# A decoder stack on one core: four attention units in flight in owned PSUM bank pairs, and projection pairs split in equal halves

## The reference, cut to what matters

```python
# first block, per layer (x: 512 x 1024)
h = rmsnorm(x, g_mix)
dq, dk, dv, c_q, c_kv_kr, xq, gate_logits = split(h @ w_in)
y_diff = diff_attention(...)    # 8 heads, 2 softmax maps each, causal; out = map0 @ v - lam * map1 @ v
y_mla  = latent_attention(...)  # 8 heads of 96, queries and keys from a latent projection, causal
y_mem  = memory_cross_attention(...)  # 4 heads of 128 over 256 rows of memory, no mask
x = x + (sum of gates * (y @ w_o)) @ w_out
x = x + square(relu(rmsnorm(x) @ w_mlp1)) @ w_mlp2
# second block, per layer
p = split(rmsnorm(x) @ w_in)
# four mixers: sparse attention with an index of chosen keys (dsa), attention in three
# branches (compressed keys, selected, windowed), a short convolution, pooled means
x = x + (concatenation of the four, each gated) @ w_out
```

## Time and profile before

| what | value |
|---|---|
| median of 3 executions | 3046.03 us (3041.13 to 3048.8) |
| the profiled execution, its own time | 3044.45 us |
| its span in the profile | 3042.7 us |
| PE, matmul | 2788.1 us busy (92%) |
| POOL | 1955.5 us (64%) |
| DVE | 1165.3 us (38%) |
| ACT | 732.8 us (24%) |
| mean granted TensorE clock | 0.961 of full speed |

### The profile page before, as it was taken

How to read it: one execution, slowest core, us unless ns; L and a number is a source line. 1 busy time by engine, 2 the same in 40 slices (tenths; PEclk the granted TensorE clock), 3 DMA queues, 4 the chain that set the end, 5 groups by cost and what they waited for, 6 DMA issues and landing times. The chain is left out here.

```text
span 3042.7 us, 38827 instructions
## 1 busy us (share of the span) xinstructions
PE 2788.1 (92%) x14268; PEld 2256.7 (74%) x14268; DVE 1165.3 (38%) x1936; ACT 732.8 (24%) x1417; POOL 1955.5 (64%) x1562
## 2 busy tenths in 40 slices
PE   6988999999899997989899999899998999989997
PEld 5766777778788886667777778788887876777765
DVE  4278273311210113278173320310012387426773
ACT  3220454200130201221365210220111114212250
POOL 5767421788798895877420788788896772266704
PEclk9999999999999998999899999999998999989998
DMA  4312100233233333322100233223333321042202
GB/s 120 94 52 66 51 8 8 80 94 96 72 96 97 95 96 82 106 70 67 54 8 1 70 87 97 80 87 96 96 97 88 92 77 32 28 93 73 80 1 69
DMA packets 158902, 217.26 MB, mean 71 GB/s; under 512 B 51312, under 2 KB 62832, under 8 KB 158704
## 3 DMA queue, kind: packets, MB, share of 16 engines
q1 hardware_dynamic: 119952, 209.72, 23.6%
q10 hardware_dynamic: 38752, 4.95, 1.3%
HBM read 212.52 MB, written 2.10 MB: 71 GB/s over the span
## 5 line engine op out<-in xcount | busy, mean ns | idle before, releaser
L290 POOL TENSOR_TENSOR weight_parts<-weight_ring,zero 128x512 fp32r<-128x512 f32 x760 | 863.4, 1136 | 853.4 <-PE ps L375 453.0
L293 POOL TENSOR_TENSOR weight_parts<-weight_ring,weight_parts 128x512 fp32r<-128x512 f32 x780 | 1077.7, 1382 | 62.8 <-ACT weight_parts L301 2.6
L377 PE MATMUL ps<-h_feature_major_high,weight_parts 128*128 128x512 f32 x2304 | 584.6, 393 | 19.5 <-DVE h_feature_major_low L471 6.6
L377 PEld LDWEIGHTS ps<-h_feature_major_high,weight_parts 128*128 128x128 f32 x2304 | 430.4, 189 | 124.8 <-POOL weight_parts L290 11.2
L375 PE MATMUL ps<-weight_parts,h_feature_major_high 128*128 128x512 f32 (+1 forms) x1920 | 463.0, 381 | 34.5 <-DVE h_feature_major_low L1613 9.1
L375 PEld LDWEIGHTS ps<-weight_parts,h_feature_major_high 128*128 128x128 f32 x1920 | 341.8, 194 | 119.0 <-issue 21.9
L377 PE MATMUL ps<-h_feature_major_low,weight_parts 128*128 128x512 f32 x1152 | 309.4, 390 | 0.0
L375 PE MATMUL ps<-weight_parts,ut_high 128*128 128x512 f32 x1024 | 254.6, 390 | 0.0
L377 PEld LDWEIGHTS ps<-h_feature_major_low,weight_parts 128*128 128x128 f32 x1152 | 216.9, 188 | 45.8
L375 PE MATMUL ps<-weight_parts,h_feature_major_low 128*128 128x512 f32 (+1 forms) x960 | 239.1, 376 | 0.0
L507 PE MATMUL ps<-arena 64*128 64x512 f32 (+9 forms) x704 | 172.9, 488 | 56.0 <-ACT probs L563 23.1
(11 more groups left out here) (231 smaller groups left out, 2930.7 us busy)
## 6 DMA issues: line engine op xcount, KB each, us to landing
weight_ring<-in_w_in SPq DMA_DIRECT2D x344, 256.0 KB, 2.7
weight_ring<-in_w_mlp SPq DMA_DIRECT2D x256, 256.0 KB, 2.7
weight_ring<-in_w_out SPq DMA_DIRECT2D x64, 256.0 KB, 2.6
weight_ring<-in_w_mem_kv SPq DMA_DIRECT2D x32, 256.0 KB, 2.9
weight_ring<-in_w_diff_o SPq DMA_DIRECT2D x32, 256.0 KB, 2.6
weight_ring<-in_w_mla_o SPq DMA_DIRECT2D x16, 256.0 KB, 2.6
weight_ring<-in_w_cross_o SPq DMA_DIRECT2D x16, 256.0 KB, 2.6
arena<-in_mem SPq DMA_DIRECT2D x2, 1024.0 KB, 5.2
```

What stands on the lines that cost most here:

```text
L290: self.nc.gpsimd.tensor_tensor(high, raw, self.m["zero"][:].broadcast_to([P, raw.shape[1]]), ALU.add).then_inc(self.s["slab_high"], 1)
L293: self.nc.gpsimd.tensor_tensor(low, raw, high.bitcast(F32), ALU.subtract).then_inc(self.s["slab_split"], 1)
L377: last = self.nc.tensor.matmul(banks[:, t, :], w[:, cut], h, **ends)
```

## The change: four units in flight, and equal halves

Each unit owns the pair of banks 2(u%4), 2(u%4)+1. Scores, transposes and the weighted result are written to the same pair one after the other (`pair`, `result`). `turn` moves to three rounds behind the scores and stands ahead of `scores` in a round; `copy` moves with it. `probs` gets a third buffer in memory that is free at that time. The waits change with the buffers. The hooks `joins` and `maps` are constant here (no unit joins, two maps). The last rounds are mixed into the next projection at slabs 1 and 3. The latent projection and the two pairs of block two are split in two equal halves (2 x 336, 2 x 340 and 2 x 326 columns).

```diff
-        parts = [(0, A.scores), (2, A.turn), (3, A.weight)]
+        parts = [(3, A.turn), (0, A.scores), (3, A.weight)]
...
-            self.first_wait[name] = (self.s["finished" if self.order.index(name) % 2 else "exped"], hi)
+            self.first_wait[name] = (self.s["finished"], hi if self.order.index(name) % 2 else hi - 2)
...
-            self.project(pe, *projection, {1 + k: f for k, f in enumerate(tail)})
+            self.project(pe, *projection, {1 + 2 * k: f for k, f in enumerate(tail)})
...
+    def pair(self, u):
+        return self.m["ps"][:, 2 * (u % 4):2 * (u % 4) + 2, :]
+    def joins(self, u):
+        return False
+    def maps(self, u):
+        return 1 if self.joins(u) else 2
+    def result(self, u):
+        return self.pair(u)[:, 1 if self.joins(u) else 0, 0:2 * P]
+    def probs(self, u):
+        return self.slots(u)
...
     def scores(self, u):
-        if u >= 2:
-            pe.wait_ge(self.s["exped"], u - 1)
+        if u >= 4:
+            pe.wait_ge(self.s["finished"], u - 3)
...
     def turn(self, u):
-        pe.wait_ge(self.s["exped"], u + 1)
-        if u >= 1:
-            pe.wait_ge(self.s["turned_copied"], u)
+        if self.joins(u):
+            pe.wait_ge(self.s["joined"], sum(map(self.joins, range(u + 1))))
+        else:
+            pe.wait_ge(self.s["exped"], u + 1)
...
     def weight(self, u):
         pe.wait_ge(self.s["turned_copied"], u + 1)
-        if u >= 2:
-            pe.wait_ge(self.s["finished"], u - 1)
...
     def exp(self, u):
         act.wait_ge(self.s["maxed"], u + 1)
-        if u >= 2:
-            act.wait_ge(self.s["turned"], u - 1)
+        if u >= 3:
+            act.wait_ge(self.s["turned"], u - 2)
...
-        "lat0": tok(w_in, C_LAT, W512), "lat1": tok(w_in, C_LAT + W512, 256),
+        "lat0": tok(w_in, C_LAT, LATW // 2), "lat1": tok(w_in, C_LAT + LATW // 2, LATW // 2),
...
+    third = [view(outs, 4096, 2, W512), view(arena, 16384, 2, W512)]
+    A = Attention(nc, m, s, units, lambda u: m["probs"][:, u % 3] if u % 3 < 2 else third[u >= U2])
...
-            A.steps(U1, U2, (2, A.copy), (0, A.exp), between={prep_rounds[-2]: lambda: roots(st_both)})
+            A.steps(U1, U2, (3, A.copy), (0, A.exp), between={prep_rounds[-2]: lambda: roots(st_both)})
...
+            act.wait_ge(s["weighted"], U2)
...
-        "za0": tok(w_in, 0, W512), "za1": tok(w_in, W512, 256),
-        "zb0": tok(w_in, Z_B, W512), "zb1": tok(w_in, Z_B + W512, 256),
+        "za0": tok(w_in, 0, A_W // 2), "za1": tok(w_in, A_W // 2, A_W // 2),
+        "zb0": tok(w_in, Z_B, B_W // 2), "zb1": tok(w_in, Z_B + B_W // 2, B_W // 2),
...
-                sums = ps[:, 6 + n % 2, 0:2 * P].rearrange("p (j d) -> p j d", j=2)[:, :, unit["at"]:unit["at"] + HD2]
+                sums = A.result(n).rearrange("p (j d) -> p j d", j=2)[:, :, unit["at"]:unit["at"] + HD2]
```

More of the change, by code:

```diff
@@ L475, with __init__ @@
 class Attention:
-    def __init__(self, nc, m, s, units):
-        self.nc, self.m, self.s, self.units = nc, m, s, units
+    def __init__(self, nc, m, s, units, slots):
+        self.nc, self.m, self.s, self.units, self.slots = nc, m, s, units, slots
     def round(self, i, lo, hi, parts, ahead=0):
@@ L505, in scores @@
         for j in range(2):
-            bank = self.m["ps"][:, 2 * (u % 2) + j, :]
-            last = pe.matmul(bank[:, 0:a["n"]], a["q"][j], a["k"][j], start=True, stop=a["mask"] is None)
+            last = pe.matmul(self.pair(u)[:, j, 0:a["n"]], a["q"][j], a["k"][j], start=True, stop=a["mask"] is None)
         if a["mask"] is not None:
@@ L510, in scores @@
             for j in range(2):
-                bank = self.m["ps"][:, 2 * (u % 2) + j, :]
-                last = pe.matmul(bank[:, col:col + rhs.shape[1]], self.m["ident16"][:], rhs, start=False, stop=True)
+                last = pe.matmul(self.pair(u)[:, j, col:col + rhs.shape[1]], self.m["ident16"][:], rhs, start=False, stop=True)
         last.then_inc(self.s["scores"], 1)
@@ L533, in weight @@
         pe.wait_ge(self.s["turned_copied"], u + 1)
-        if u >= 2:
-            pe.wait_ge(self.s["finished"], u - 1)
         blocks, rows = max(1, a["n"] // P), min(P, a["n"])
-        for j in range(2):
+        for j in range(self.maps(u)):
             for kb in range(blocks):
-                last = pe.matmul(self.m["ps"][:, 6 + u % 2, j * P:(j + 1) * P],
+                last = pe.matmul(self.result(u)[:, j * P:(j + 1) * P],
                                  self.m["probs_t"][0:rows, u % 2, j, kb * P:(kb + 1) * P], a["v"][j](kb),
@@ L548, in maximum @@
         out = self.m["negmax"][:, u % 4, :]
[L549 to L550 removed]
+        last = dve.tensor_reduce(out, self.pair(u)[:, :, 0:a["n"]], AX.X, ALU.max, negate=True)
         if a.get("may_be_empty"):
@@ L559, in exp @@
         act.wait_ge(self.s["maxed"], u + 1)
-        if u >= 2:
-            act.wait_ge(self.s["turned"], u - 1)
+        if u >= 3:
+            act.wait_ge(self.s["turned"], u - 2)
         for j in range(2):
-            last = act.activation(self.m["probs"][:, u % 2, j, 0:a["n"]],
-                                  self.m["ps"][:, 2 * (u % 2) + j, 0:a["n"]], ACT.Exp,
+            last = act.activation(self.probs(u)[:, j, 0:a["n"]], self.pair(u)[:, j, 0:a["n"]], ACT.Exp,
                                   bias=self.m["negmax"][:, u % 4, j:j + 1],
@@ L911, in _ @@
                     scaled("mk_t", [(mkt[:, h, :], h, P, MEM, ckg) for h in range(CH)])
-            A.steps(0, U1, (2, A.copy), (0, A.exp), ahead=2)
+            A.steps(0, U1, (3, A.copy), (0, A.exp), ahead=2)
             roots(st_d[:, :, 16:32])
-            empty("lat0", lat[:, :, 0:W512])
-            empty("lat1", lat[:, :, W512:LATW], width=LATW - W512)
+            empty("lat0", lat[:, :, 0:LATW // 2], width=LATW // 2)
+            empty("lat1", lat[:, :, LATW // 2:], width=LATW // 2)
             roots(st_lat)
@@ L937, in _ @@
                 scaled(f"m_t{2 + k}", [(kmt[0:MQK, 4 * k + h, :], h, MQK, SEQ, mkg[0:MQK]) for h in range(4)])
-            A.steps(U2, U3, (2, A.copy), (0, A.exp))
+            act.wait_ge(s["weighted"], U2)
+            A.steps(U2, U3, (3, A.copy), (0, A.exp))
             roots(st_o)
@@ L1297, in block_two @@
                               v=[lambda kb: za[:, kb, A_V:A_V + P]] * 2, at=0))
-    A = Attention(nc, m, s, units)
+    third = view(arena, dup_at, 2, W512)
+    A = Attention(nc, m, s, units, lambda u: m["probs"][:, u % 3] if u % 3 < 2 else third)
     U = len(units)
@@ L1422, in _ @@
             load_small(small[1:])
-            for name, dst, at, width in (("za0", za, 0, W512), ("za1", za, W512, A_W - W512), ("zb0", zb, 0, W512), ("zb1", zb, W512, B_W - W512)):
+            for name, dst, at, width in (("za0", za, 0, A_W // 2), ("za1", za, A_W // 2, A_W // 2), ("zb0", zb, 0, B_W // 2), ("zb1", zb, B_W // 2, B_W // 2)):
                 empty(name, [(dst[:, :, at:at + width], L.banks(name)[:, :, 0:width], ACT.Copy, 1.0)])
@@ L1445, in _ @@
             empty("cmp_t", [(kcmpt, L.banks("cmp_t")[:, 0, 0:NCMP], ACT.Copy, 1.0)])
-            A.steps(0, U, (2, A.copy), (0, A.exp))
+            A.steps(0, U, (3, A.copy), (0, A.exp))
             L.square_right(act, 1, junk)
```

14 lines of the change are left out of this document (7 added, 7 removed).

## The result

The changed kernel takes **3197.89 us** (median of 4 runs, 3196.71 to 3203.82) beside 3045.70 (4 runs) for the kernel before: a ratio of **1.0505**, interval 1.0486 to 1.0524, slower. The profiled execution spans 3194.9 us against 3042.7, at a mean granted clock of 0.953 against 0.961. The forecast was 3192, within 3115 to 3245.

What follows compares the result with a forecast made beforehand. TensorE's own work plus its waits was taken as the bound. Per layer, block one adds 34+18+6.6 and block two a net 15; two layers each give +148 on 3044.45: 3192 us, range 3115 to 3245.

Steps and rivals of the forecast that it cites:

- The hand-over and its price: Differential units: scores wait for the previous unit's finish with only transposes as cover; period 15.36 us against 10.81, +1.14 a round.
- F: Attention: time from the end of a unit's weights through VectorE's finish and back to TensorE, 1.34 us in differential units.
- T: Differential units: TensorE's time for a unit's transposes, start to start: 0.22, 0.47, 0.66, 0.88 us for 128 to 512 keys.
- The lower bound: Differential units, ScalarE and VectorE never delaying the hand-over: period 13.65 us, +0.71 a round, total up some 80 to 95.
- Differential +34: Block one's differential units, per layer: eight periods of 15.36 us plus head and tail, 132.3 us against 98.56.
- Latent +18: Block one's latent units, per layer: +11 us from 11 rounds at about +0.98, and +7.4 from the tail.
- Cross +6.6: Block one's cross units, per layer: four rounds wait 0.6 us each and the tail adds 4.2, delaying VectorE's chain to L1119.
- Block two's attention +22.5: Block two, per layer: 21 rounds take 70.6 us against about 59.6, plus head +1.5, dsa rounds and tail +10.
- The clock rival: Attention: new waits lower TensorE's busy share, the clock falls to a mean of 0.85, total 3250 us; chance 0.13.
- The halves: the step that failed: Equal projection halves: -8.1 us a layer in block two; latent halves' 3.9 us lost to TensorE's wait for VectorE's rotation, zero.
- The hidden handover: Attention: finish released and done within the transposes, so old waits and 16 us of halves go, 2997 us; chance 0.05.
- Does less: Stages VectorE already bounds, perhaps block two: new waits replace old, only block one pays, about 3110 us; chance 0.14.

## Why the prediction was right

- **The hand-over and its price.** F = 1.34 from the earlier trace rows and the recurrence through the queues gave waits of 0.91, 1.12, 0.87 and 0.87 for the finish and 0.42 and 0.64 for the copy; measured 0.70, 0.96, 0.67, 0.73, and 0.27, 0.48. All six rows are 0.14 to 0.21 lower, because a row counts the idle time from the end of the last matmul (T(384) reads 0.82) and the prediction counted from start to start (0.66); so the period comes out only 0.15 below. That the hand-over is a cause is shown from both sides: with the finish covered and ahead in its queue 109 us go, and a finish shorter by 0.43 makes each of these waits shorter by 0.42 or 0.43. The copy's lost cover is the second part: given back, it takes 75 off.
- **The lower bound.** 13.65 a period with both queues out of the way; 13.80 measured. Its total of +80 to +95 isn't reached (+108), because block two didn't gain from the new queue order: 117.3 and 113.9. (Where its code is that of the changed kernel, the runs read 113.3 to 117.2.)
- **Differential +34:** +36.4 and +35.9. The eight periods give 35.2 of it (36.4 worked out); head and tail, which were to get 2.7 shorter, got about 1 longer. **Latent +18:** +17.2; its window holds 375 matmuls against 363, the slab that the tail was moved by. **Cross +6.6:** without the halves the stretch from the first cross scores to the first differential ones grew from 150.3 and 151.0 to 157.8 and 158.2, +7.4.
- **Block two's attention +22.5:** +20.5 and +24.3, right in sum and not in its parts. TensorE's idle time grew from 6.1 to 19.6 and 18.9, by 13; the other 7 to 11 are matmuls in flight for longer, at a granted clock of 0.88 and 0.84 in place of 0.93. The waits were oversized and the clock filled the gap.
- **The clock rival** came true in part. Some groups run at the lower level of 1.2 GHz also in the differential stage, which had a clock of 0.98 before and has 0.94. In the 8 us before the first row TensorE had been idle for 0.74, 1.24 and 0.27 us (timeline of TensorE and a window, kernel after):

```profile
393.89 0.64 PE L545 MATMUL ps<-ident,probs 128*128 128x128 f32 x2
395.27 1.65 PE L526 MATMUL ps<-arena 64*128 64x384 f32 x4 [0.75 <-DVE outs L1104]
```

```profile
393.00:401.00 8.00, 6.79 (x32) 4.71 (x30) 6.22 (x11) 3.14 (x9) 0.00 (x0) 0.58 0.00 0
```

  The same scores take 0.92 at 462.88. A mean of 0.953 against 0.961 is 9.4% of 3194.9 us at the lower level against 7.8% of 3042.7, 63 us more, of which under half, some 25 us (an estimate), is lost. The Trainium skill (TensorE: Matmul & The Clock Gate, A second HAM failure mode) describes a swing between the two levels with short idle gaps between groups of matmuls; this trace agrees, with gaps of 0.3 to 1.2 us, where the prediction said that no row showed it. A fall to 0.85 everywhere it is not. What the prediction gave for this rival, "the stage with the lower share has the lower clock", was misread from the earlier trace rows: block two has the higher share of busy time there, 86.70 of 92.80 (93%) against 88.15 of 98.56 (89%), and the lower clock.
- **The halves: the step that failed.** Block two's -8.1 a layer was right (8.5 alone; 7.0 in the changed kernel, where that stretch is 248.3). "The time that the equal halves save [...] is swallowed by this wait: zero here" was wrong, and with it the sign "with a longer wait of L389 for it". The start and the length of the chain in front of L1119 were taken as not touched by the halves. Both moved: with the halves alone it starts 2.2 sooner and is 1.8 shorter, and TensorE's wait for it goes from 7.51 to 4.0. In the changed kernel the wait is 4.9, without the halves 8.5. Counted from the first cross scores, L389 starts 88.4 us on before, 92.9 in the changed kernel and 94.6 without the halves: the 6 to 7 that attention was to add are there (6.2), and the halves take 1.8 of them back.
- **The balance.** Attention 167 in these windows (162 predicted), halves and the rest -15 (-15 predicted): +152 on the profiled execution, +148 forecast. That the total comes within 6 us is in part luck: the halves gave 4 to 8 more than their price, attention cost 5 more, and the two nearly cancelled.
- **The rivals.** The hidden handover (2997) needed F below T; no such round is in the timeline. "Does less" was wrong: block two paid in full, if partly through the clock.

## What to carry to other kernels

When each unit of a pipeline owns its buffers for its whole life, the hand-over that frees them moves onto the engine's own order: write down, for each of the three hand-overs (exponentials, copy, finish), which of the engine's steps lie between the giving step and the waiting one, and compare them with the latency of a row. With a fixed number of steps a round, cover that one hand-over gains another loses. And a narrower tile can bring a chain on another engine to its end sooner, by starting it sooner or by getting out of its way: a cover isn't a constant, if it shares something with what the change makes smaller.

## What the runs showed of the hardware that was not expected

- VectorE's operations on 512 columns take 1.23 and 1.24 us beside POOL's 336-column splits and 1.37 and 1.77 beside its 512-column ones, and the two engines go in step. A scaling of 384 columns takes 0.41 us with POOL idle and 1.51 beside its splits.
- TensorE's clock fell to the lower level inside a stage that is 73% busy with no wait above 2.0 us, for a few rounds at a time and not in every period of the same pattern. What decides it stays open.
